# The order of the two token tiles inside a score visit: second tile first for two of three attention branches

## What is computed

```python
s = jnp.einsum('bqhd,bkhd->bhqk', qb, k).astype(jnp.float32) * scale      # MLA: 96 dims, FoX: 64 dims
if cum_k is not None:
    s = s + (cum_q[..., :, None] - cum_k[..., None, :])                   # FoX: forget-gate decay
s = jnp.where(key_pos[None, :] <= q_pos[:, None], s, -jnp.inf)
p = jax.nn.softmax(s, axis=-1).astype(v.dtype)
...
s = jnp.einsum('bqhd,bqkd->bhqk', qb, k_sel).astype(jnp.float32) * scale  # sparse branch: 64 dims, shared keys
s = s - slopes[None, :, None, None] * dist[:, None]
```

## Time and profile before

| | |
|---|---|
| three executions | 838.88, 838.98, 839.54 us; median 838.98 us |
| span of the profiled execution, first to last instruction | 838.7 us |
| TensorE (PE) busy | 826.2 us, 99% of the span |
| TensorE weight loads (PEld), overlapping | 770.9 us, 92% |
| VectorE (DVE) busy | 605.2 us, 72% |
| ScalarE (ACT) busy | 464.1 us, 55% |
| GpSimd (POOL) busy | 113.8 us, 14% |
| granted TensorE clock, mean | 0.998 |

### The profile page before, as it was taken

The page is one execution under the profiler, slowest core; times in us unless marked ns, Lnnn a source line. Parts: engine busy times, 40 slices in busy tenths (PEclk is TensorE's granted clock), DMA queues, the critical chain, the costliest instruction groups (busy, mean ns, idle before and its releaser), DMA issues.

```text
span 838.7 us, 15687 instructions
## 1 busy us (share of the span) xinstructions
PE 826.2 (99%) x6326; PEld 770.9 (92%) x6326; DVE 605.2 (72%) x1076; ACT 464.1 (55%) x701; POOL 113.8 (14%) x133
## 2 busy tenths in 40 slices
PE   7999999999999999999999999999999999999996
PEld 6899999999899999988889998998998999999885
DVE  5675788987786877765676568888797687777554
ACT  5675866663456655543447576756545475555440
POOL 1503910006300000000000067000180000000000
PEclk9999999999999999999999999999999999999999
DMA  9959643344579766475847694443467767764731
GB/s 307 240 131 280 192 137 117 136 152 151 165 189 240 197 193 184 160 244 175 267 114 190 127 333 118 145 131 122 151 185 198 190 190 195 200 189 151 250 115 50
DMA packets 190265, 150.98 MB, mean 180 GB/s; under 512 B 32653, under 2 KB 164337, under 8 KB 189937
## 3 DMA queue, kind: packets, MB, share of 16 engines
q1 hardware_dynamic: 181120, 143.09, 57.9%
q10 hardware_dynamic: 9072, 6.90, 3.0%
HBM read 148.63 MB, written 1.06 MB: 178 GB/s over the span
## 4 chain that ended last, share of the span: by engine, by line
PE 92%; DMA 2%; DVE 2%; POOLq 1%; SPq 1%; ACT 1%; ACTq 1%; POOL 1%; issue 0%; DVEq 0%
PE ps L672 28%; PE ps L674 27%; PE ps L673 27%; PE ps L955 3%; PE ps L986 2%; PE ps L967 2%; POOLq L1989 1%; DMA decay<-decay_rows 1%; DMA raw<-w_in 1%; PE ps L730 1%; DVE w_lo L1499 1%; ACTq L1203 0%; ACT w_hi L1154 0%; PE ps L1052 0%; POOL rel_first L1986 0%
## 5 line engine op out<-in xcount | busy, mean ns | idle before, releaser
L1499 DVE TENSOR_TENSOR w_lo<-raw,w_hi 128x2048 fp32r<-128x2048 f32 (+2 forms) x140 | 303.2, 2167 | 111.5 <-ACT w_hi L1154 111.4
L672 PE MATMUL ps<-xt_hi,w_hi 128*128 128x256 f32 x1232 | 344.9, 280 | 0.0
L673 PE MATMUL ps<-xt_lo,w_hi 128*128 128x256 f32 x1232 | 340.6, 276 | 0.0
L674 PE MATMUL ps<-xt_hi,w_lo 128*128 128x256 f32 x1232 | 340.5, 276 | 0.0
L1154 ACT ACTIVATE w_hi<-raw 128x2048 fp32r<-128x2048 f32 (+3 forms) x142 | 253.0, 1786 | 77.9 <-PE ps L674 71.0
L672 PEld LDWEIGHTS ps<-xt_hi,w_hi 128*128 128x128 f32 x1232 | 231.3, 188 | 3.3 <-issue 2.0
L673 PEld LDWEIGHTS ps<-xt_lo,w_hi 128*128 128x128 f32 x1232 | 231.7, 188 | 0.0
L674 PEld LDWEIGHTS ps<-xt_hi,w_lo 128*128 128x128 f32 x1232 | 231.3, 188 | 0.0
L672 PE MATMUL ps<-w_hi,ht_hi 128*128 128x512 f32 x176 | 68.6, 390 | 0.0
L674 PE MATMUL ps<-w_hi,ht_lo 128*128 128x512 f32 x176 | 68.5, 389 | 0.0
L673 PE MATMUL ps<-w_lo,ht_hi 128*128 128x512 f32 x176 | 68.5, 389 | 0.0
(11 more groups left out here) (252 smaller groups left out, 1276.1 us busy)
## 6 DMA issues: line engine op xcount, KB each, us to landing
raw<-ffn_w_up SPq DMA_DIRECT2D x88, 512.0 KB, 5.2
raw<-w_in SPq DMA_DIRECT2D x84, 512.0 KB, 5.5
raw<-ffn_w_down SPq DMA_DIRECT2D x32, 512.0 KB, 4.0
raw<-w_branch SPq DMA_DIRECT2D x24, 512.0 KB, 4.4
raw<-w_out SPq DMA_DIRECT2D x16, 512.0 KB, 4.6
raw<-ffn_w_down SPq DMA_DIRECT2D x24, 256.0 KB, 3.0
decay<-decay_rows ACTq DMA_DIRECT2D x2, 1024.0 KB, 8.6
ln_g<-ln_g ACTq DMA_DIRECT2D x4, 512.0 KB, 3.5
```

The lines of the kernel that those rows point to most:

```text
L672: pe.matmul(dst, a_hi, b_hi, start=first, stop=False)
L673: pe.matmul(dst, a_hi, b_lo, start=False, stop=False)
L674: return pe.matmul(dst, a_lo, b_hi, start=False, stop=last)
L1499: ins = dve.tensor_tensor(low, panel_raw(l, p)[0:n, cols], panel_hi(l, p)[0:n, cols].bitcast(F32), ALU.subtract)
```

## The change

In the FoX and the sparse branch the loop over token tiles inside a score visit runs backwards: the products of the second tile (256 keys) of both heads are issued before those of the first tile (128 keys). MLA keeps its order. `scores_ready` is still raised by the last product issued, which is now that of the first tile, head 1.

```diff
-                for t in range(NT):
+                for t in range(NT) if b == MLA else reversed(range(NT)):
                     for a in range(2):
```

## The result

The changed kernel takes 840.88 us (median of 11 runs, 840.60 to 841.40), the kernel before 838.98 us (11 runs, 838.80 to 839.63). The ratio is 1.0021 with a 95% interval of 1.0014 to 1.0029: 1.90 us slower, outside the forecast range of 838.4 to 839.9 us.

What follows compares the result with a forecast made beforehand. TensorE was taken to bound the kernel; in each of 16 visits the front's 0.10 us loss is given back at the exit, summing to 0.00 us on the 838.98 us median. Forecast 839.0 us, range 838.4 to 839.9 us.

Steps and rivals of the forecast that it cites:

- What bounds the kernel: Whole kernel: TensorE in flight 826.2 of 838.7 us, 92% of the last chain; 13 to 16 changed visits count in full.
- The visit step by step: FoX or sparse score visit: steps of 0.21, 0.31, 0.22, 0.11 and 0.21 us after, 1.06 us before and after.
- no dearer front: Visit's first step stays about 0.22 us while the exit falls to 0.21: 1.4 to 1.6 us faster, 837.4 us; chance 2%.
- a broken pair: Visit's front: long product keeps the second head out, 0.44 us a visit, 7.0 us over 16, 846.0 us; chance 2%.
- no cheaper exit: Visit's exit to the whole array stays at 0.31 us, so the front's 0.10 us is lost: 1.6 us, 840.6 us; chance 2%.
- who waits for the visit: Behind the visit: scores end at 103.12 us as before, transposes start at the same time, so nothing downstream moves.
- the change is worth 0.00 us in a visit: FoX and sparse visits: front loses 0.10 us, exit gives it back; -0.3 to +0.3 us over 16 visits.
- The bounds: Visit's third step, short behind long: 0.10 to 0.12 us, taken as 0.11; 0.02 us to either side in a visit.
- The lower end of the range: Forecast time: 838.4 us, from 838.98 less 0.3 from the steps and less the allowed spread of runs.
- The comparison of times: Kernel before: profiled span 838.7 us taken as 0.3 us under the 838.98 us median of the runs.
- The slower rivals: Visit's front or exit: pair breaks up, 846.0 us, or exit stays dear, 840.6 us; 2% each, 0.03 for over 0.2% slower.
- The third one: Rival at the visit's exit: switch back to the whole array keeps 0.31 us, 1.6 us slower, 840.6 us; chance 2%.

Runs made afterwards that it cites:

- second profile: The kernel before, with no edit, run and profiled once more beside the kernel before: median 839.97 us against 839.75 us, ratio 1.0002.
- first mixed order: Kernel before with FoX and sparse products ordered tile 1 head 0, tile 0 head 1, tile 0 head 0, tile 1 head 1: 839.09 against 839.48 us, ratio 0.9998.

## Why the prediction was wrong

- **What bounds the kernel** was right. The chain stays on TensorE (93%), and what TensorE loses in the slots moves the end; in the changed profile all 16 visits lie on it.
- **The visit step by step** was right. All five steps came out within 0.01 us of what was read from the index and value products, and the sum is 1.06 us; the rivals that priced a step otherwise (no dearer front, a broken pair, no cheaper exit) did not occur. In ns, behind a fast tile, the visit became shorter, 1059 to 1060 where it was 1062 to 1063.
- **The step that failed** is the last sentence on who waits for the visit, "nothing downstream, the next visit's wait included, has a reason to move", and with it "the change is worth 0.00 us in a visit", carried to 16 visits. The visit gained 2 to 4 ns and the first transpose behind it up to 2 more, which brought the hand-over from 1693 or 1694 to 1689 ns, and behind every hand-over of 1689 or 1690 ns the tile was slow (50 of 50). That put 164 triples at 353 instead of 340 ns, a term of 2.2 us where the sum had nothing. The forecast treated the products behind a visit as having one price, whereas in the very trace read for it 258 triples stood at the slow one (from 32 to 52 us, behind the values of each layer's end at 194 and 605 us, and from about 230 to 260, 450 to 470 and 640 to 670 us). I read the starts inside the visits closely and did not read them in the tiles, which hold most of the chain.
- **The bounds** were those of a visit's own steps, 0.02 us each. An error of 0.004 us in a visit was inside them and cost 0.14 us behind it (1.9 us over the 14 visits with transposes). The lower end of the range, 838.4 us, is not what its terms give either (838.98 - 0.3 - 0.56 = 838.1), which changes nothing here.
- **The comparison of times** was off: the profiled execution of before was not 0.3 us under the median but an execution of about 840.5 us.
- **The slower rivals** got 0.03 for the right sign by the wrong mechanism. The third one's 840.6 us lies near the measured time by coincidence: the exit that it held at 0.31 us fell to 0.21. That a nearly unchanged visit can change the pace of what follows was not among the rivals.
- **Where the loss is a little smaller than the count.** 163 triples make 2.2 us, and 1.9 us were measured. The end of the slots gave some back: in the changed kernel the branch products from 194 to 214 us ran fast in the profile where they had been slow before. Between the slots and 225 us the slow triples fell from 54 to 15, and at the same place of the second layer from 54 to 41. In the profiles the stretch from the first layer's slots to the second's is 0.36 us shorter (313.17 and 312.81 us) and the one from there to the end 0.14 us (241.53 and 241.39 us), 0.5 us in all; the same stretches of the kernel before, its second profile and the first mixed order spread by 0.3 us, so this account is rough. In the first layer the chain then lies there on GpSimd's additions, where it lay on TensorE before, so that part of the gain is not paid out:

```profile
200.98 3.61 POOL merged L1999 x3
...
206.51 2.58 POOL merged L1999
...
213.34 2.52 POOL merged L1999
```

No version that beats both kernels came out of this. The first mixed order is level with the kernel before.

## What to carry to other kernels

A long stream of equal products has to be checked for its pace before and after an edit, by the mean ns of its groups in a window; a change that leaves every edited instruction at its price can still alter the price of the hundreds behind it. Where an edit is worth nothing by its own sum, a stream that now runs at its fast pace can lose it, as in the slots, and one at the slow pace can gain it, as behind them. Profiles of single executions that differ by 1 to 2 us are compared stretch by stretch, from one landmark to the next, never by their spans.

## What the runs showed of the hardware

- Full-array products of 256 columns in a dense stream ran at two paces that last until the next interruption, 113.3 and 117.8 ns start to start (340 and 353.3 ns for three), at the same granted clock (0.997 to 0.999 on average in all runs). A weight load starts within 5 ns of the preceding product's start in both.
- The pace is fixed within the first few products behind an interruption. Behind a fast tile no length of the hand-over led to both paces in the 225 cases of the table: 1689, 1696, 1798 and 1802 to 1805 ns slow, 1693, 1800 and 2001 ns fast. The lengths of 1696, 1800, 1805, 1864, 2000 and 2076 ns stand on one or two cases each. Behind a slow tile the length did not decide (2006 ns led to both).
- What makes the two paces, and why a few ns decide between them, is not shown by these runs; operands at other addresses were not tried.
- The execution enters the slots at 87.7 to 89.4 us from its start in the profiles of kernels whose work up to there is the same; single spans spread by as much for that alone.
